# Two heads per unit in the memory and sparse attention of a fused transformer kernel

## The reference, cut to what matters

```
def memory_xattn(h, mem_n, wq, wk, wv, wo):
    q = (h @ wq).reshape(b_, s_, XA_HEADS, XA_HEAD_DIM)
    k = (mem_n @ wk).reshape(b_, m_, XA_HEADS, XA_HEAD_DIM)
    v = (mem_n @ wv).reshape(b_, m_, XA_HEADS, XA_HEAD_DIM)
    s = jnp.einsum('bthd,bmhd->bhtm', q, k).astype(F32) * (XA_HEAD_DIM ** -0.5)
    prob = jax.nn.softmax(s, axis=-1).astype(v.dtype)
    o = jnp.einsum('bhtm,bmhd->bthd', prob, v).reshape(b_, s_, XA_WIDTH)
    return o @ wo
...
# dsa_mix: sel holds the 64 latent rows c_kv that the index picks for a query
s = jnp.einsum('bthc,btkc->bthk', ql, sel).astype(F32) * (DSA_HEAD_DIM ** -0.5)
s = jnp.where(valid[:, :, None, :], s, -jnp.inf)
prob = jax.nn.softmax(s, axis=-1).astype(sel.dtype)
return jnp.einsum('bthk,btkc->bthc', prob, sel)
```

## Time and profile before

| | |
|---|---|
| median of 3 runs | 2538.91 us (2538.68 to 2539.89) |
| the profiled execution | 2539.36 us, its span 2537.5 us |
| mean granted PE clock over the span | 0.917 of full |
| first memory attention, first score to first output matmul | 1583.62 to 1607.80: 24.18 us |
| sparse attention, first score to first L1070 | 2162.73 to 2196.95: 34.22 us |
| second memory attention, first score to first output matmul | 2276.74 to 2300.59: 23.85 us |

### The profile page before, as it was taken

How to read it: one execution, slowest core, us unless ns; L and a number is a source line. 1 busy time by engine, 2 the same in 40 slices (tenths; PEclk the granted TensorE clock), 3 DMA queues, 4 the chain that set the end, 5 groups by cost and what they waited for, 6 DMA issues and landing times.

```text
span 2537.5 us, 42838 instructions
## 1 busy us (share of the span) xinstructions
PE 2259.9 (89%) x17670; PEld 2180.3 (86%) x17670; DVE 1483.9 (58%) x2119; ACT 940.7 (37%) x1227; POOL 19.5 (1%) x32
## 2 busy tenths in 40 slices
PE   6789999999989999999945958899999996788997
PEld 6679999888979999999934958799999995588997
DVE  5545755556546755755767645477467446564773
ACT  3333434333343434443311114444334332433442
POOL 0000000000000000000000000000000000000000
PEclk8889999999999999999967959799999977898998
DMA  6223553433323553554510013145445532141452
GB/s 238 100 84 117 198 184 143 147 117 133 118 82 119 196 185 125 188 195 154 199 44 0 1 48 135 64 169 186 162 149 193 188 132 80 56 140 54 178 189 80
DMA packets 48508, 334.42 MB, mean 132 GB/s; under 512 B 5632, under 2 KB 7424, under 8 KB 8448
## 3 DMA queue, kind: packets, MB, share of 16 engines
q1 hardware_dynamic: 46080, 323.36, 35.5%
q10 hardware_dynamic: 2304, 9.24, 1.1%
HBM read 331.53 MB, written 1.05 MB: 131 GB/s over the span
## 4 chain that ended last, share of the span: by engine, by line
PE 78%; DVE 11%; issue 9%; ACT 2%; POOL 0%; DMA 0%; DVEq 0%; SPq 0%; POOLq 0%; ACTq 0%
PE pj L226 14%; PE pj L227 13%; PE pj L228 13%; PE acc L226 6%; PE acc L227 6%; PE acc L228 6%; PE mb L334 3%; PE acc L523 2%; PE pj L234 2%; PE pj L232 2%; PE pj L233 2%; PE acc L515 2%; PE mb L532 1%; DVE sm L558 1%; PE mb L355 1%
## 5 line engine op out<-in xcount | busy, mean ns | idle before, releaser
L302 DVE TENSOR_TENSOR wlo<-raw,whi 128x2048 fp32r<-128x2048 f32 x299 | 685.2, 2292 | 445.9 <-ACT whi L295 445.8
L226 PE MATMUL pj<-xh,whi 128*128 128x256 f32 x3024 | 880.2, 291 | 48.7 <-DVE xl L379 33.0
L227 PE MATMUL pj<-xl,whi 128*128 128x256 f32 x3024 | 872.9, 289 | 0.0
L228 PE MATMUL pj<-xh,wlo 128*128 128x256 f32 x3024 | 872.2, 288 | 0.0
L295 ACT ACTIVATE whi<-raw 128x2048 fp32r<-128x2048 f32 x299 | 569.7, 1909 | 583.9 <-PE acc L228 256.5
L226 PEld LDWEIGHTS pj<-xh,whi 128*128 128x128 f32 x3024 | 599.1, 198 | 56.6 <-issue 53.9
L227 PEld LDWEIGHTS pj<-xl,whi 128*128 128x128 f32 x3024 | 599.0, 198 | 0.0
L228 PEld LDWEIGHTS pj<-xh,wlo 128*128 128x128 f32 x3024 | 598.3, 198 | 0.0
L226 PE MATMUL acc<-AR,whi 128*128 128x256 f32 (+1 forms) x1376 | 393.1, 286 | 12.1 <-DVE AR L1661 7.0
L227 PE MATMUL acc<-AR,whi 128*128 128x256 f32 (+1 forms) x1376 | 389.9, 283 | 0.0
L228 PE MATMUL acc<-AR,wlo 128*128 128x256 f32 (+1 forms) x1376 | 389.4, 283 | 0.0
(11 more groups left out here) (308 smaller groups left out, 2300.5 us busy)
## 6 DMA issues: line engine op xcount, KB each, us to landing
raw<-in_wstream SPq DMA_DIRECT2D x302, 1024.0 KB, 4.8
F<-in_rpb SPq DMA_DIRECT2D x4, 1024.0 KB, 15.9
F<-in_memtok ACTq DMA_DIRECT2D x2, 1024.0 KB, 4.8
F<-in_memin ACTq DMA_DIRECT2D x2, 1024.0 KB, 6.9
F<-in_small ACTq DMA_DIRECT2D x1, 1536.0 KB, 6.6
xT<-in_xin SPq DMA_DIRECT2D x2, 512.0 KB, 6.5
F<-in_consts ACTq DMA_DIRECT2D x1, 1024.0 KB, 4.7
out<-xT SPq DMA_DIRECT2D x8, 128.0 KB, 2.1
```

What stands on the lines that cost most here:

```text
L226: nc.tensor.matmul(o, wh, k_hi, start=first, stop=False, skip_group_check=True)
L227: nc.tensor.matmul(o, wh, k_lo, start=False, stop=False, skip_group_check=True)
L228: return nc.tensor.matmul(o, wl, k_hi, start=False, stop=last, skip_group_check=True)
L302: nc.vector.tensor_tensor(wlo[:, gs, :], raw[:, gs, :], whi[:, gs, :].bitcast(F32), ALU.subtract).then_inc(w_lo, 1)
```

## The change

Units in memory and sparse attention become two heads by one half of the tokens, 4 and 8 of them. Their scores go into `acc[0]` and `acc[1]` for even units and into `pj[0]` and `pj[1]` for odd units, so scores(u) still waits for `sm` of unit u-2. A group is two heads; its output fills a whole bank (`o_pair`), and finish moves 512 columns at once. `per` is the number of heads in a group and scales the `od` counts; it is 1 in the other two attentions, which stay as they are.

```diff
-                "dil": {**attn(32, 8), "oh": 8}, "xa": {**attn(8, 4), "oh": 4}, "dsa": attn(16, 8), "rwrt": {}}
+                "dil": {**attn(32, 8), "oh": 8}, "xa": {**attn(4, 4, 2), "oh": 4}, "dsa": attn(8, 8, 2), "rwrt": {}}
...
+        def score_bank(u, U, i):
+
+            if U["H"] == 1:
+                return acc[u % 2]
+            if U["per"] == 2:
+                return ((acc[0], acc[1]), (pj[0], pj[1]))[u % 2][i]
+            return acc[i]
+
...
-                back = 2 if U["H"] == 1 else 1
+                back = 2 if U["H"] == 1 or U["per"] == 2 else 1
...
-                    b = acc[u % 2 if U["H"] == 1 else i]
+                    b = score_bank(u, U, i)
...
-                    pe.wait_ge(*at(tag, "od", U["grp"] + 1 - deep))
+                    pe.wait_ge(*at(tag, "od", U["per"] * (U["grp"] + 1 - deep)))
...
-                    x = U["soft"][a](S[:, a * n:(a + 1) * n], acc[u % 2 if H == 1 else a][:, 0:n])
+                    x = U["soft"][a](S[:, a * n:(a + 1) * n], score_bank(u, U, a)[:, 0:n])
...
-        def o_bank(grp):
-            return (mb, pj[2])[grp % 2][:, 0:T]
...
+        def o_pair(grp):
+            return (mb, pj[2])[grp % 2]
+
+        def two_heads(q, k, v_, soft, t, grp):
+            return dict(scores=[(q(2 * grp + a, t), k(2 * grp + a), 0, T) for a in range(2)],
+                        pv=[(v_(2 * grp + a, j), a * T + j * P, o_pair(grp)[:, a * T + t * P:a * T + (t + 1) * P],
+                             j == 0, j == 1) for a in range(2) for j in range(2)],
+                        nk=2 * T, H=2, soft=[soft(t)] * 2, grp=grp, per=2, end=t == 1)
...
+            units = [two_heads(lambda h, t: Q[:, h, t * P:(t + 1) * P], lambda h: Kb[:, h, :],
+                               lambda h, j: V[:, j, h * P:(h + 1) * P],
+                               lambda t: lambda S, ps: nc.vector.tensor_scalar(S, ps, P ** -0.5, None, ALU.mult), t, g)
+                     for g in range(2) for t in range(2)]
...
+            def hi_f(grp):
+                nc.scalar.activation(pair_of(AR, grp), o_pair(grp)[:, :], ACT.Copy).then_inc(sg(tag, "oh"), 2)
+
+            def lo_f(dve):
+                def f(grp):
+                    dve.wait_ge(*at(tag, "oh", 2 * grp + 2))
+                    nc.vector.tensor_tensor(pair_of(AR[:, 8:12], grp), o_pair(grp)[:, :],
+                                            pair_of(AR, grp).bitcast(F32), ALU.subtract).then_inc(sg(tag, "od"), 2)
+                return f
...
+            units = [two_heads(lambda h, t: QL[:, ql(h), t * P:(t + 1) * P], lambda h: CQ[:, 2, :],
+                               lambda h, j: CT[:, j, :],
+                               lambda t: lambda s_, ps: nc.vector.scalar_tensor_tensor(
+                                   s_, ps, 64 ** -0.5, MBs[:, t, :], ALU.mult, ALU.add), t, g)
+                     for g in range(DH // 2) for t in range(2)]
...
-                    nc.scalar.activation(OL[:, grp, :], o_bank(grp), ACT.Copy).then_inc(sg(tag, "od"), 1)
+                    nc.scalar.activation(OL[:, 2 * grp:2 * grp + 2, :].rearrange("p a t -> p (a t)"),
+                                         o_pair(grp)[:, :], ACT.Copy).then_inc(sg(tag, "od"), 2)
```

More of the change, by code:

```diff
@@ L618, in attn_act, with split_out @@
             fin(u0 + len(units) - 1, units[-1])
-        def o_bank(grp):
-            return (mb, pj[2])[grp % 2][:, 0:T]
-        def split_out(tag, perm, o_bank=o_bank):
+        def o_pair(grp):
[5 more added lines that the diff above has]
+                        nk=2 * T, H=2, soft=[soft(t)] * 2, grp=grp, per=2, end=t == 1)
+        def split_out(tag, perm, o_bank):
             def dst(a):
@@ L786, in na_units @@
                         S, ps, HD ** -0.5, b, ALU.mult, ALU.add) for a in range(2)]
-                    out_.append(dict(scores=sc, pv=pv, nk=2 * T, H=2, soft=soft, grp=grp, end=t == 1))
+                    out_.append(dict(scores=sc, pv=pv, nk=2 * T, H=2, soft=soft, grp=grp, per=1, end=t == 1))
                 return out_
@@ L802, in dil_units @@
                         S, DM[:, t, :], slopes[:, h:h + 1], ps, ALU.mult, ALU.add)]
-                    out_.append(dict(scores=sc, pv=pv, nk=512, H=1, soft=soft, grp=grp, end=hp_ == 1 and t == 1))
+                    out_.append(dict(scores=sc, pv=pv, nk=512, H=1, soft=soft, grp=grp, per=1, end=hp_ == 1 and t == 1))
                 return out_
@@ L904, in xattn, with pair_of @@
             V = take(2, XH * P)
-            hi_f, lo_f = split_out(tag, False)
             mt = tag + "m"
[L908 to L913, removed]
+            units = [two_heads(lambda h, t: Q[:, h, t * P:(t + 1) * P], lambda h: Kb[:, h, :],
+                               lambda h, j: V[:, j, h * P:(h + 1) * P],
+                               lambda t: lambda S, ps: nc.vector.tensor_scalar(S, ps, P ** -0.5, None, ALU.mult), t, g)
+                     for g in range(2) for t in range(2)]
+            def pair_of(a, grp):
+                return a[:, 2 * grp:2 * grp + 2, :].rearrange("p a t -> p (a t)")
+            def hi_f(grp):
[6 more added lines that the diff above has]
+                return f
             def pe_f(pe, w):
```

## The result

The changed kernel takes 2520.88 us (median of 4 runs, 2520.0 to 2521.65) against 2539.4 of the kernel before in the same runs; the ratio is 0.9927, 95% interval 0.991 to 0.9944. That is 18.5 us, where I forecast 7.3 and a lowest time of 2527.5. The span of the profiled execution fell from 2537.5 to 2519.7 us, by 17.8.

The account below looks back on a forecast made before the run. PE is busy 89% of the span, so only stretches where PE waits can give time. Sparse attention 4.3 and two memory attentions 1.5 each sum to 7.3 us, giving 2531.6 us; range 2527.5 to 2536.8.

Parts of the forecast that it names:

- The round: Loop over DVE and PE for two heads: 3.02 us at full clock against 3.86, DVE waiting 0.82 for PE.
- Sparse attention: Built up to 29.5 us against 34.22, 4.7 less; 4.3 less taken, bounds 3.3 and 5.6.
- two rounds at half clock, + 6.94: Sparse attention: the two rounds after the first softmaxes run at half clock and add 6.94 us.
- The tail: End of sparse attention, from the last scaling through transposes, values and finish: 3.98 us.
- nearer the row: Sparse attention: 4.3 us taken instead of 4.7, because half-clock PE was still behind by some values when the clock rose.
- Memory attention: Each of the two: 1.5 us less, bounds 0 and 2.7; built up as 20.04 us at half clock, 15.81 at full.
- I expect less full clock than before: Memory attention: fewer, longer PE gaps in only four units mean less full clock, so 1.5 us each was taken.
- the far end: Memory attention: 4.8 us less if the clock is full throughout.
- The sum over the kernel: Whole kernel: 4.3 + 2 x 1.5 = 7.3 us less, giving 2531.6 us.
- the clock stays high: Rival: denser PE raises the clock sooner; sparse 5.1 and memory 3.0 each, 11.1 us less, 2527.8; chance 0.20.
- The coarse pipeline: Rival: fill, the 5.05 us of finish and tail eat memory attention's gain; sparse gives 3.3 to 4.3, 2535.2 us; chance 0.21.
- `score_bank` at nothing: Score banks: keeping the distance of two units costs nothing; with `acc[0:2]` alone scores would wait a round.

Follow-up runs that it names:

- experiments 2, 5 to 9: 2: two heads a unit in memory attention only, 2527.07 us; 5 to 8: dummy matmuls before sparse stage, old kernel, 2534.07 to 2539.09; 9: four, changed kernel, 2526.46.
- experiment 11: Changed kernel with dummy matmuls: one ahead of second memory attention, 934.9 us from first scores to end for 934.7; or one in each PE wait, 2518.0 us.

## Why the prediction was wrong

- **The round:** right. 3.01 us for 3.02, DVE's wait 0.82 for 0.82.
- **Sparse attention:** 5.39 for 4.3 taken, inside its bounds of 3.3 and 5.6. The term that was mis-sized is "two rounds at half clock, + 6.94": the clock rose after 6.0 us instead of 9.9. At full clock they would have been 6.04, and that is 0.9 of the 1.1 us between 4.3 and 5.39. The tail, from the last L574 (2176.15) to the first L1089 (2180.46), is 4.31 us for 3.98, 0.3 longer. The built-up sum gave 4.7; taking 4.3 "nearer the row" moved it the wrong way.
- **Memory attention:** 4.41 and 0.97 for 1.5 each. Both built-up sums hold: from the first softmax to the output projection 16.2 us at full clock (15.8 predicted) and 19.7 at half clock (20.0 predicted). The step that failed is the choice between them, "I expect less full clock than before": the first got more (0.91 for 0.68) and the second less (0.63 for 0.75). The first exceeds the bound of 2.7 and stays within what I called the far end, 4.8. Half-clock rounds came as predicted too: 3.47 us, with a wait of DVE of 1.28 for 1.27.
- **The sum over the kernel:** this is the step that took the time out of the range. I added the three attentions and held all else constant. 7.0 us came from elsewhere, 5.0 of them in the two stretches ahead of sparse attention, through the clock (experiments 2, 5 to 9). With 10.8 alone the time would have been about 2528, within the range, near the rival "the clock stays high" (11.1). That nearness is luck: the rival had 3.0 for each memory attention, and 4.41 and 0.97 came.
- **The coarse pipeline:** the finish wait is there and as large as said (3.81 and 5.09 us). It cost 2.4 and 2.9 us, as moving it showed, but didn't eat the gain. The Trainium skill (Perfetto Trace Analysis, Optimizing Scalar/DVE Operations) gives larger operations as a gain if the engine is saturated. DVE was not: 58% of the span (the prediction's 59% is a slip) and 59% of the sparse attention. Here the measurement decides: larger units shortened the loop over DVE and PE by 0.85 us for two heads at full clock (3.01 for 3.86). About half of that, 0.47, is DVE's own part (2.19 for 2.66), which the larger operations made cheaper, and 0.38 is one trip to PE of 0.82 us in place of two of 0.60. DVE's part counted although the engine was not full, since it stands in the loop.
- **`score_bank` at nothing:** as an edit that keeps a distance it was right. What it is worth was named wrongly, a round of waiting; it is 0.20 us a round at full clock, 1.1 at half (4.57 for the 3.47 of memory attention with alternation), and with the lower clock 18.6 us over the three attentions.

Open: why the clock takes one decision or the other at a given place. I can reproduce it, not compute it. The 3.12 us between the first memory attention and the norm ahead of the sparse stage are clock, as PE's busy time shows, but they aren't one decision: 0.9 us less behind the attention (clock 1.00 for 0.94), then stretches of 0.6 less, 1.4 more, 1.5 less and 1.6 less.

## What to carry to other kernels

When two engines hand a tile to and fro and neither is full, count the length of the loop, not the busy shares: the trips, and each engine's own part between them. Twice the tile for one trip took a fifth off it, about half by the trip saved and half by cheaper operations. Look also at the order of what stands in front of the next trip: in memory attention moving the finish was worth more than the larger units. An edit that shifts a stretch by a few microseconds can move unchanged stages behind it by 5 us through PE's clock, so a difference of that size is only the edit's own if the touched stretches show it; a shift by dummy matmuls ahead of the stage tells the two apart. Judge such a shift by the time to the end of the kernel, since the stage behind can give the gain back, as in experiment 11. Where PE waits in short gaps at half clock, giving it work in the gaps may be cheaper than leaving it idle; here it cost at most 0.33 us an attention, and the one gain, of 3.5 us, isn't proven to come from it.

## What the runs showed of the hardware that I had not expected

PE's clock fell to half while the profile shows PE busy all the time. Windows of PE alone in the kernel before and then in the kernel after, in the projection of the sparse stage (busy, clock, DMA):

```profile
2048.00:2054.00 6.00, 6.00 (x52) 1.00 0.97 336
2054.00:2057.00 3.00, 3.00 (x27) 0.92 0.69 289
2057.00:2072.00 15.00, 15.00 (x71) 0.50 0.22 71
2072.00:2075.00 3.00, 2.84 (x18) 0.73 0.00 0
```

```profile
2048.00:2054.00 6.00, 6.00 (x56) 1.00 0.61 245
2054.00:2057.00 3.00, 3.00 (x19) 0.60 0.75 270
2057.00:2063.00 6.00, 6.00 (x29) 0.50 0.11 42
2063.00:2066.00 3.00, 3.00 (x20) 0.69 0.00 0
```

In both, the fall comes within or just behind the norm's 32 matmuls of one column (from 2054.43 before, from 2049.59 after). From the shares in the windows at either end, half clock lasts some 17 us before and some 10 after. Most of that time PE runs small matmuls still: behind the norm come 48 of eight columns, until 2069.43 before and 2061.94 after, and only then those of 256. Timeline of PE before, the first and the last of eight columns and the first of 256:

```profile
2059.19 0.35 PE L232 MATMUL pj<-whi,xh 128*128 128x8 f32 x1
...
2069.22 0.35 PE L234 MATMUL pj<-wlo,xh 128*128 128x8 f32 x1
2069.43 0.56 PE L226 MATMUL pj<-xh,whi 128*128 128x256 f32 x1
```

The clock rises about 4 us into those of 256 columns before, and about 3 us after. It rises later before because it fell earlier among the small matmuls: after, the first 13 of the 48 still ran at full clock, and before, none did. At half clock one of eight columns takes 0.21 us, as much as one of 256; at full clock it takes 0.11.

And the executions agreed more than they had reason to. They reach the first memory attention up to 5.3 us apart (1580.65 to 1585.97 in the seventeen profiles), and yet the stretches behind repeat within 0.2 us where the code up to there is the same (a profile shows one execution of each kernel; the kernel before has two). The Trainium skill (TensorE: Matmul & The Clock Gate, What's actually happening) calls the window of the clock gate free-running, not reset by the kernel. With an independent rhythm a shift of the whole by some microseconds should change the stretches as the dummy matmuls did; it doesn't here. Something ahead of the first memory attention seems to align the two, and no run shows what.
